# The first tap of the feed-forward convolution, for the first token group, on ScalarE out of PSUM

## The chip, the cores and the metric

One core of a Trainium2 chip. The metric is the device time of one launch in microseconds; lower is better. The kernel is written by hand, engine by engine, with semaphores between the engines; nothing reorders it afterwards.

## The reference, cut to what matters

Two decoder layers run over 1024 prompt tokens and 32 sample tokens (8 sequences of 4). Each layer has a mixer, a norm, a feed-forward block with a causal convolution of width 3, and a norm. The second layer's mixer holds a sparse attention: an indexer scores keys, the best 256 per query are kept, and the rest is masked. The change touches the feed-forward block:

```
def causal_dwconv(ext, w):
    t = ext.shape[1] - (CONV_W - 1)
    out = ext[:, CONV_W - 1:] * w[CONV_W - 1]
    for j in range(CONV_W - 1):
        out = out + ext[:, j:j + t] * w[j]
    return out

def conv_ffn(x, hist, w_up, conv_w, conv_b, w_down):
    hu = x @ w_up
    ext = jnp.concatenate([hist, hu], axis=1)
    hc = causal_dwconv(ext, conv_w) + conv_b
    y = (jax.nn.silu(hc[..., :D_FF]) * hc[..., D_FF:]) @ w_down
    return y, ext[:, -(CONV_W - 1):]
```

D_MODEL is 1024 and D_FF is 2816, that is 22 chunks of 128 channels (FC in the kernel), each with a half that goes through silu (j = 0) and a half that multiplies it (j = 1). `w[2]` is the tap on the token itself, and it is the first that the kernel takes, with the bias.

## The kernel before, in words

**Layout and groups.** Channels lie on the 128 partitions and tokens along the row. The tokens form two groups: GA, the first 512 prompt tokens, and GB, the other 512 and the 32 samples (544 columns). GA runs through a feed-forward block in one pass, GB in the next. The four passes are numbered pz: 0 (layer 0, GA), 1 (layer 0, GB), 2 (layer 1, GA), 3 (layer 1, GB). Beside pass 0 runs the norm of GB, row by row. Beside pass 2 run group B's sample attention, the indexer's scores and top-k, and prompt attention heads in pairs.

**Slabs.** Weights are streamed in slabs of 128x1024 or less. SyncE loads them into a ring of three buffers RAW. ScalarE rounds a slab to the high part WH (split_high, L1029), called by `ahead`, two slabs before PE needs it. GpSimd subtracts to get the low part WL (L1448). PE makes three matmuls per chunk of 128 (high by high at L606, low by high at L607, high by low at L609) into one of two slots of PSUM, which alternate. It takes a slot again when `evac_done` of that slot says that it was emptied.

**One pass.** A pass has blocks of 4, 6, 6 and 6 chunks. A block has two up slabs for each chunk (j = 0, then j = 1) and then 8 down slabs, so 8 + 8, 12 + 8, 12 + 8 and 12 + 8 slabs, numbered 0 to 75 below. An up slab's result, 128 channels by 512 tokens, takes this way:

- ScalarE copies it from PSUM to a row `ext` (L1148), behind two columns of history, and this frees the slot. The rows are extB0 and extB1 in passes 0, 1 and 3, and extA0 and extA1 in pass 2.
- VectorE makes the three taps in `taps`: `cv = ext * w2 + bias` (L1725, TENSOR_SCALAR), then adds `ext * w0` and `ext * w1` (L1729 and L1731, SCALAR_TENSOR_TENSOR). In a trace a tap is a line cvA or cvB.
- With j = 1, ScalarE takes silu of the j = 0 half (L1155), VectorE multiplies the halves to hf (L1847), and in the next slab but one ScalarE rounds hf to HH or HHA (`hidden_high`, L1123) and VectorE keeps the rest in HL or HLA (L1835) for the down slabs.

The taps' numbers and the bias are in `fpar[:, 2 * c + j, 0:4]`, in memory on the chip. At the start of pass 0 ScalarE itself issues the loads of fpar0 and of fhist (the samples' history); VectorE waits for `fpar_in` before its first tap. fpar1, for layer 1, is loaded before the end of the second pass.

**Order.** Each engine has its own list of steps. `beside(s, 0)` and `beside(s, 1)` put other work in front of or behind a slab's own: the norm's rows in pass 0 (ScalarE L1116 and L1117 write XLF and XH from Z, VectorE L1814 scales, GpSimd L1492 subtracts and adds in Z), the indexer's R (ScalarE L1181 and L1183) and SC (GpSimd L1503), the top-k (VectorE L2038 and L2040) and the pair steps in pass 2. A pair step has the row maxima of two heads' scores (VectorE L2059), exponentials (ScalarE L1225), the reciprocal of their sums (VectorE L2064), the scaled probabilities PRB (ScalarE L1229), and PE's transposition of them (L870), which stands between two slabs in PE's list. ScalarE loads a table of functions (ACT_TABLE_LOAD) when silu and the exponential alternate.

Of the kernel before, what the change touches and what calls it, by code (L numbers as in the profile page):

```python
# [173 lines left out]
def build(nc, io):  # L174
    with ExitStack() as ctx:
# [354 lines left out]
        def ffn_blocks(pz):  # L530

            n, c, out = PASSES[pz], 0, []
            for nb in BLOCKS:
                out.append((n, nb, c))
                n, c = n + 2 * nb + KD, c + nb
            return out
# [481 lines left out]
        def _(act):  # L1018
# [106 lines left out]
            def ffn(pz, q_norm):  # L1125

                layer, gr = pz // 2, pz % 2
                ext, cv = ffn_place(pz)[0:2]
                if pz == 0:
                    act.wait_ge(mm_done, F0[0])  # L1130
                    act.dma_start(fpar0[:, :, :], io["fpar"][0]).then_inc(fpar_in, 16)
                    act.dma_start(fhist[:, :, :, :], io["fhist"][0]).then_inc(fpar_in, 16)
                if pz == 2:
                    act.wait_ge(sc_acc, 32)
                    act.wait_ge(edge_zero, 4)
                for n, nb, c0 in ffn_blocks(pz):
                    for q in range(nb):
                        c = c0 + q
                        for j in range(2):
                            s = n + 2 * q + j  # L1140
                            u = 2 * FC * pz + 2 * c + j
                            beside(s, 0)
                            ahead(s)
                            act.wait_ge(mm_done, s + 1)
                            act.wait_ge(conv_done, u + 1)
                            act.wait_ge(st_done, u + 1)
                            for dst, src_ in zip(group_parts(ext[s % 2], gr, HIST), slot_parts(s)):
                                ins = act.activation(dst, src_, ACT.Copy)  # L1148
                            ins.then_inc(evac_done[s % 2], 1)
                            if j == 0 and q:  # L1150
                                hidden_high(pz, q - 1, c - 1)
                            if j == 1:
                                act.wait_ge(conv_done, u + 2)
                                w = EXTG[gr] - HIST
                                act.activation(cv[0][:, 0:w], cv[0][:, 0:w], ACT.Silu).then_inc(silu_done, 1)  # L1155
                            beside(s, 1)
                    n += 2 * nb
                    hidden_high(pz, nb - 1, c0 + nb - 1)
                    for m in range(KD):
                        beside(n + m, 0)  # L1160
                        ahead(n + m)
                        if c0 + nb == FC:
                            square(q_norm, m)
                        beside(n + m, 1)
                if gr == GB:
                    act.wait_ge(st_done, 2 * FC * (pz + 1) + 2)
                    act.dma_start(io["o_fst"][layer], fst[:, :, :]).then_inc(fst_out, 16)
# [477 lines left out]
        def _(dve):  # L1645
# [73 lines left out]
                dve.tensor_tensor(cf[:, :], cf[:, :], U[:, g, :], ALU.mult).then_inc(gate_f, 1)  # L1719
                mix_rest(g)  # L1720

            def taps(row, out, w, taps_w, tap_sem, value, done):

                if len(taps_w) == 4:
                    dve.tensor_scalar(out, row[:, 2:2 + w], taps_w[2], taps_w[3], ALU.mult, ALU.add).then_inc(tap_sem, 1)  # L1725
                else:
                    dve.tensor_scalar(out, row[:, 2:2 + w], taps_w[2], None, ALU.mult).then_inc(tap_sem, 1)
                dve.wait_ge(tap_sem, value + 1)
                dve.scalar_tensor_tensor(out, row[:, 0:w], taps_w[0], out, ALU.mult, ALU.add).then_inc(tap_sem, 1)  # L1729
                dve.wait_ge(tap_sem, value + 2)  # L1730
                dve.scalar_tensor_tensor(out, row[:, 1:1 + w], taps_w[1], out, ALU.mult, ALU.add).then_inc(done, 1)  # L1731

            for jj in range(4):
                n = 8 + 3 * jj
                dve.wait_ge(mm_done, n + 2)
                wait_emptied(dve, n)
                dve.wait_ge(bstd, jj + 1)
                for dst, src_, c in zip(parts(bext, HIST), bank_parts((n + 1) % 2), parts(cf)):
                    ins = dve.tensor_tensor(dst, src_, c, ALU.mult)
                ins.then_inc(evac_done[(n + 1) % 2], 1)  # L1740
                wait_emptied(dve, n + 1)
                dve.wait_ge(bhist, jj + 1)
                taps(bext, bcv[:, :], CW, [bw[:, jj, t:t + 1] for t in range(3)], btap, 2 * jj, bconv)
                dve.wait_ge(bconv, jj + 2)
                dve.wait_ge(mm_done, n + 3)
                conv_parts = [bcv[:, 0:2 * TW].rearrange("p (c t) -> p c t", c=2), bcv[:, 2 * TW:NP],
                              sample_cols(bcv, 0, HIST + DEC, DEC, NP)]
                for dst, src_, c in zip(parts(cf), bank_parts(n % 2), conv_parts):
                    ins = dve.tensor_tensor(dst, src_, c, ALU.mult)
                ins.then_inc(evac_done[n % 2], 1)  # L1750
                mix_rest(4 + jj)
# [97 lines left out]
            def ffn(pz, q_norm):  # L1849
# [8 lines left out]
                for n, nb, c0 in ffn_blocks(pz):  # L1858
                    for q in range(nb):
                        c = c0 + q  # L1860
                        for j in range(2):
                            s, local = n + 2 * q + j, 2 * c + j
                            u = 2 * FC * pz + local
                            beside(s, 0)
                            wait_emptied(dve, s)
                            if gr == GB:
                                dve.wait_ge(ext_hist, 2 * FC * layer + local + 1)
                            if j == 0 and FC * pz + c:
                                dve.wait_ge(hmul, FC * pz + c)
                            taps(ext[j], cv[j][:, 0:w], w, [fpar[:, local, t:t + 1] for t in range(4)], tap, 2 * u, conv_done)  # L1870
                            if j == 0 and q:
                                hidden_rest(pz, q - 1, c - 1)
                            if j == 1:
                                hidden(pz, c)
                            beside(s, 1)
                    n += 2 * nb
                    hidden_rest(pz, nb - 1, c0 + nb - 1)
                    for m in range(KD):
                        beside(n + m, 0)
                        projected(n + m, m, c0 == 0, c0 == 0)  # L1880
                        if c0 + nb == FC:
                            summed(q_norm, m)
                        beside(n + m, 1)
# [421 lines left out]
```

## Time and profile before

| what | value |
|---|---|
| time, 3 runs | median 2978.38 us (2977.19 to 2985.26) |
| the profiled execution's own time | 2971.72 us |
| its span | 2969.7 us |
| PE busy | 2655.3 us (89%) |
| VectorE (DVE) busy | 1606.8 us (54%) |
| ScalarE (ACT) busy | 1078.2 us (36%) |
| GpSimd (POOL) busy | 1242.6 us (42%) |
| chain that ended last | PE 63%, DVE 16%, ACT 7%, issue 5%, POOL 4% |

Times in the trace are microseconds from the start of the span; the profiled execution's time is 2 us more than its span. Busy time is what an engine's instructions took, their stalls among it. "Chain that ended last" follows the program back from its last instruction, at each step to what released it. A row of a timeline gives an instruction's start, its duration, the engine and line, the operation and its tiles, and in brackets how long the engine was idle in front of it and what ended that. PEclk is the clock granted to PE as a share of 2.4 GHz.

### The profile page before, as it was taken

The page shows a single profiled execution, that of the slowest core. Times are in us where ns is not written, and L with a number is a line of the kernel's source. Part 1 is how long each engine was busy: PE and PEld are TensorE (multiplying, and loading weights), DVE is VectorE, ACT ScalarE, POOL GpSimd, SP SyncE. Part 2 cuts the span into 40 slices and gives each one's busy share as a digit, 9 for nine tenths or more (in the row PEclk, how much of TensorE's full clock was granted, in tenths as well). Part 3 has the DMA queues.
Part 4 walks back from the last instruction along what each step waited for, and adds up shares of the span by engine and source line. Part 5 has one row for each costly group of instructions (what it writes and reads, how often), then busy time and mean ns, then how long its engine had stood idle before and what let it go on. Part 6 is the DMA issues. An engine that isn't in the chain of part 4 may idle for free.

```text
span 2969.7 us, 39274 instructions
## 1 busy us (share of the span) xinstructions
PE 2655.3 (89%) x15720; PEld 2254.1 (76%) x15720; DVE 1606.8 (54%) x2392; ACT 1078.2 (36%) x1732; POOL 1242.6 (42%) x1026
## 2 busy tenths in 40 slices
PE   7989988999979999989879669797889898899997
PEld 7989876878879999857768434355566667799997
DVE  3332575354564334567763368588994434553434
ACT  2111343333333223343234253155354543432333
POOL 2212444444455555465323341154222224554554
PEclk9999998999989999989889779899999999899998
DMA  3101222323222222312211314331111113132232
GB/s 125 43 30 58 86 67 75 93 93 98 86 64 81 91 92 80 109 51 83 97 54 62 108 33 134 117 128 41 59 54 61 57 55 118 48 96 86 82 95 80
DMA packets 96096, 235.44 MB, mean 79 GB/s; under 512 B 10442, under 2 KB 31498, under 8 KB 95530
## 3 DMA queue, kind: packets, MB, share of 16 engines
q1 hardware_dynamic: 85344, 210.95, 22.6%
q10 hardware_dynamic: 10570, 21.97, 2.0%
q8 instruction: 125, 2.05, 0.3%
q14 instruction: 57, 0.47, 0.1%
HBM read 219.43 MB, written 13.45 MB: 78 GB/s over the span
## 4 chain that ended last, share of the span: by engine, by line
PE 63%; DVE 16%; ACT 7%; issue 5%; POOL 4%; DMA 2%; SPq 1%; ACTq 0%; DVEq 0%; POOLq 0%
PE PS L606 19%; PE PS L609 18%; PE PS L607 18%; DVE SC L2038 3%; POOL WL L1448 2%; DMA RAW<-in_slabs 2%; POOL SC L1503 2%; ACT WH L1029 1%; DVE m8b L2040 1%; PE PS L816 1%; PE PS L852 1%; PE PS L795 1%; ACT XH L1117 1%; PE PS L870 1%; DVE m8a L2040 1%
## 5 line engine op out<-in xcount | busy, mean ns | idle before, releaser
L1448 POOL TENSOR_TENSOR WL<-RAW,WH 128x1024 fp32r<-128x1024 f32 (+2 forms) x400 | 885.7, 2215 | 1571.8 <-ACT WH L1029 1571.4
L606 PE MATMUL PS<-XH,WH 128*128 128x272 f32 (+2 forms) x3312 | 1076.5, 335 | 70.4 <-POOL WL L1448 32.5
L607 PE MATMUL PS<-XL,WH 128*128 128x272 f32 (+2 forms) x3312 | 1055.6, 329 | 0.0
L609 PE MATMUL PS<-XH,WL 128*128 128x272 f32 (+2 forms) x3312 | 882.8, 329 | 0.0
L606 PEld LDWEIGHTS PS<-XH,WH 128*128 128x128 f32 x3312 | 639.1, 193 | 143.9 <-issue 47.4
L607 PEld LDWEIGHTS PS<-XL,WH 128*128 128x128 f32 x3312 | 639.2, 193 | 41.4 <-issue 1.7
L1029 ACT ACTIVATE WH<-RAW 128x1024 fp32r<-128x1024 f32 (+2 forms) x400 | 388.0, 970 | 771.2 <-DMA RAW<-in_slabs 764.6
L609 PEld LDWEIGHTS PS<-XH,WL 128*128 128x128 f32 x3312 | 567.9, 192 | 43.4
L1725 DVE TENSOR_SCALAR cvB<-extB,fpar 128x560 f32<-128x560 f32 (+1 forms) x132 | 109.2, 827 | 395.3 <-ACT extB L1148 392.4
L606 PE MATMUL PS<-HH,WH 128*128 128x272 f32 (+1 forms) x880 | 265.2, 316 | 25.5 <-POOL WL L1448 18.0
L607 PE MATMUL PS<-HL,WH 128*128 128x272 f32 (+1 forms) x880 | 262.8, 313 | 0.0
L609 PE MATMUL PS<-HH,WL 128*128 128x272 f32 (+1 forms) x880 | 218.4, 313 | 0.0
L606 PEld LDWEIGHTS PS<-HH,WH 128*128 128x128 f32 x880 | 169.0, 192 | 38.8 <-POOL WL L1448 21.9
L1768 DVE TENSOR_TENSOR Z<-Z,PS 128x512 f32<-128x512 f32 (+1 forms) x96 | 67.5, 704 | 221.9 <-PE PS L609 221.9
L607 PEld LDWEIGHTS PS<-HL,WH 128*128 128x128 f32 x880 | 168.8, 192 | 8.1
L1148 ACT ACTIVATE extB<-PS 128x240 f32<-128x240 f32 (+3 forms) x308 | 92.2, 362 | 177.9 <-PE PS L609 177.9
L609 PEld LDWEIGHTS PS<-HH,WL 128*128 128x128 f32 x880 | 146.8, 192 | 7.8
L1729 DVE SCALAR_TENSOR_TENSOR cvB<-extB,fpar,cvB 128x560 f32<-128x560 f32 (+1 forms) x132 | 111.4, 844 | 4.7
L1731 DVE SCALAR_TENSOR_TENSOR cvB<-extB,fpar,cvB 128x560 f32<-128x560 f32 (+1 forms) x132 | 108.1, 819 | 4.7
L1492 POOL TENSOR_TENSOR Z<-Z,sqb 128x512 f32<-128x512 f32 (+1 forms) x64 | 95.1, 1504 | 13.7 <-ACT sqb L1095 13.7
L1765 DVE SCALAR_TENSOR_TENSOR Z<-Z,PS 128x512 f32<-128x512 f32 (+1 forms) x64 | 45.0, 704 | 90.0 <-PE PS L609 89.1
L1116 ACT ACTIVATE XLF<-Z,lnp 128x512 f32<-128x512 f32 (+1 forms) x48 | 39.6, 826 | 147.7 <-DVE Z L1814 147.7
(281 smaller groups left out, 3328.7 us busy)
## 6 DMA issues: line engine op xcount, KB each, us to landing
RAW<-in_slabs SPq DMA_DIRECT2D x272, 512.0 KB, 3.5
RAW<-in_slabs SPq DMA_DIRECT2D x96, 384.0 KB, 3.0
RAW<-in_slabs SPq DMA_DIRECT2D x32, 256.0 KB, 2.9
KP<-in_ck SPq DMA_DIRECT2D x32, 256.0 KB, 3.2
VP<-in_cv SPq DMA_DIRECT2D x32, 256.0 KB, 2.9
xb_rows<-spill ACTq DMA_DIRECT2D x8, 272.0 KB, 2.1
Z<-xb_rows ACTq DMA_DIRECT2D x1, 2176.0 KB, 12.6
out_o_y<-Z ACTq DMA_DIRECT2D x4, 544.0 KB, 2.8
```

The source lines that it names most:

```text
L606: pe.matmul(o, WH[n % 3][:, k, :], hi(k)[:, c], start=first, stop=False)
L607: pe.matmul(o, WH[n % 3][:, k, :], lo(k)[:, c], start=False, stop=False)
L609: mm = pe.matmul(o, WL[n % 3][:, k, :], hi(k)[:, c], start=False, stop=last)
L1029: act.activation(WH[n % 3][:, 0:kc, :], RAW[n % 3][:, 0:kc, :], ACT.Copy).then_inc(w_hi, 1)
L1148: ins = act.activation(dst, src_, ACT.Copy)
L1448: pool.tensor_tensor(WL[n % 3][:, 0:kc, :], RAW[n % 3][:, 0:kc, :], WH[n % 3][:, 0:kc, :].bitcast(F32), ALU.subtract).then_inc(w_lo, 1)
L1492: pool.tensor_tensor(z, z, LNS[q][3][:, :], ALU.subtract).then_inc(ln_sub, 1)
L1725: dve.tensor_scalar(out, row[:, 2:2 + w], taps_w[2], taps_w[3], ALU.mult, ALU.add).then_inc(tap_sem, 1)
L1729: dve.scalar_tensor_tensor(out, row[:, 0:w], taps_w[0], out, ALU.mult, ALU.add).then_inc(tap_sem, 1)
L1731: dve.scalar_tensor_tensor(out, row[:, 1:1 + w], taps_w[1], out, ALU.mult, ALU.add).then_inc(done, 1)
L1768: dve.tensor_tensor(by_bank(z, gr), by_bank(z, gr), slot(n), ALU.add).then_inc(evac_done[n % 2], 1)
L2038: dve.match_replace(SC[b], m8[x][:, :], SC[b], TAKEN).then_inc(top_, 1)
```

## The change

For the groups GA (passes 0 and 2, 88 up slabs) ScalarE makes the first tap itself. Right behind its copy of a slab's result it reads the same slot of PSUM once more and writes `cv[j] = slot * w2 + bias` as an Identity activation whose scale and bias are read from fpar. It waits first for `hmul`, so that the last chunk's halves in cv have been multiplied, and the slot is freed by this second instruction. For that ScalarE waits for `fpar_in` ahead of each such pass. VectorE makes the two other taps only; `taps` is cut in two. Passes 1 and 3 keep all three taps on VectorE.

```
                 ext, cv = ffn_place(pz)[0:2]
+                fpar = (fpar0, fpar1)[layer]
                 if pz == 0:
                     act.wait_ge(mm_done, F0[0])
...
+                if gr == GA:
+                    act.wait_ge(fpar_in, 48 if layer else 32)
                 for n, nb, c0 in ffn_blocks(pz):
...
                                 ins = act.activation(dst, src_, ACT.Copy)
+                            if gr == GA:
+                                act.wait_ge(hmul, FC * pz + c)
+                                ins = act.activation(cv[j][:, 0:HALF], slot(s), ACT.Identity,
+                                                     scale=fpar[:, 2 * c + j, 2:3], bias=fpar[:, 2 * c + j, 3:4])
                             ins.then_inc(evac_done[s % 2], 1)
...
-            def taps(row, out, w, taps_w, tap_sem, value, done):
+            def first_tap(row, out, w, taps_w, tap_sem, value):
 
                 if len(taps_w) == 4:
                     dve.tensor_scalar(out, row[:, 2:2 + w], taps_w[2], taps_w[3], ALU.mult, ALU.add).then_inc(tap_sem, 1)
                 else:
                     dve.tensor_scalar(out, row[:, 2:2 + w], taps_w[2], None, ALU.mult).then_inc(tap_sem, 1)
-                dve.wait_ge(tap_sem, value + 1)
+                dve.wait_ge(tap_sem, value)
+
+            def other_taps(row, out, w, taps_w, tap_sem, value, done):
+
                 dve.scalar_tensor_tensor(out, row[:, 0:w], taps_w[0], out, ALU.mult, ALU.add).then_inc(tap_sem, 1)
-                dve.wait_ge(tap_sem, value + 2)
+                dve.wait_ge(tap_sem, value)
                 dve.scalar_tensor_tensor(out, row[:, 1:1 + w], taps_w[1], out, ALU.mult, ALU.add).then_inc(done, 1)
...
-                            taps(ext[j], cv[j][:, 0:w], w, [fpar[:, local, t:t + 1] for t in range(4)], tap, 2 * u, conv_done)
+                            taps_w = [fpar[:, local, t:t + 1] for t in range(4)]
+                            if gr == GB:
+                                first_tap(ext[j], cv[j][:, 0:w], w, taps_w, tap, 6 * FC * layer + 2 * FC + 2 * local + 1)
+                            other_taps(ext[j], cv[j][:, 0:w], w, taps_w, tap,
+                                       6 * FC * layer + (local + 1 if gr == GA else 2 * FC + 2 * local + 2), conv_done)
```

How it moves instructions on ScalarE at the start of pass 0, before and then with the change (fpar_99 is fpar0, WH_61 the high part of slab 2, extB_102 the row of slab 0, cvB_104 its taps):

```order
L1131 DMA fpar_99<-in_fpar 128x176 [waits slab_multiplied]
L1132 DMA fhist<-in_fhist 128x704
L1029 ACTIVATE WH_61<-RAW_55 128x1024 [waits slab_loaded2]
L1148 ACTIVATE extB_102<-PS 128x512 [waits ffn_state,ffn_conv,slab_multiplied]
L1095 ACTIVATE sqb_214<-PS 128x544 [waits squares_summed,ln_mean_spread]
L1101 ACTIVATE stats<-stats,epst 68x8 [waits ln_var]
```

```order
L1132 DMA fpar_99<-in_fpar 128x176 [waits slab_multiplied]
L1133 DMA fhist<-in_fhist 128x704
L1029 ACTIVATE WH_61<-RAW_55 128x1024 [waits slab_loaded2,ffn_params_in]
L1151 ACTIVATE extB_102<-PS 128x512 [waits ffn_state,ffn_conv,slab_multiplied]
L1154 ACTIVATE cvB_104<-PS,fpar_99 128x512 [waits ffn_hidden]
L1095 ACTIVATE sqb_214<-PS 128x544 [waits squares_summed,ln_mean_spread]
L1101 ACTIVATE stats<-stats,epst 68x8 [waits ln_var]
```

The wait for the parameters (ffn_params_in) stands in front of the split of slab 2, and the tap behind the copy.

ScalarE around a pair step in the last block of pass 2, slab 58 (extA_160 is its row, HHA_201 the first rounded hidden row of the block, PRB the pair's probabilities), before and then with the change:

```order
L1029 ACTIVATE WH_59<-RAW_53 128x1024 [waits slab_loaded0]
L1148 ACTIVATE extA_160<-PS 128x512 [waits ffn_state,ffn_conv,slab_multiplied]
L1123 ACTIVATE HHA_201<-hfA 128x512 [waits ffn_hidden]
L1225 ACT_TABLE_LOAD [waits pa_turned]
L1225 ACTIVATE PRB,psm<-PS,nmx 128x896 [waits pa_max]
```

```order
L1029 ACTIVATE WH_59<-RAW_53 128x1024 [waits slab_loaded0]
L1151 ACTIVATE extA_160<-PS 128x512 [waits ffn_state,ffn_conv,slab_multiplied]
L1154 ACTIVATE cvA_162<-PS,fpar_154 128x512 [waits ffn_hidden]
L1123 ACTIVATE HHA_201<-hfA 128x512 [waits ffn_hidden]
L1232 ACT_TABLE_LOAD [waits pa_turned]
```

The tap stands ahead of the hidden row's rounding and of the table load for the exponentials; it and the rounding wait for the same semaphore (ffn_hidden is hmul).

VectorE around the pair step at slab 40 (SC_158 are the indexer's scores, m8a and m8b the maxima that the top-k takes out), before and then with the change:

```order
L2040 MAX m8b<-SC_158 128x8 [waits i_top]
L2059 TENSOR_REDUCE nmx<-PS 128x1 [waits pa_logits] x2
L1725 TENSOR_SCALAR cvA_162<-extA_160,fpar_154 128x512 [waits ffn_hidden,banks_emptied0]
L1729 SCALAR_TENSOR_TENSOR cvA_162<-extA_160,fpar_154,cvA_162 128x512 [waits ffn_tap]
L1731 SCALAR_TENSOR_TENSOR cvA_162<-extA_160,fpar_154,cvA_162 128x512 [waits ffn_tap]
L1835 TENSOR_TENSOR HLA<-hfA,HHA_202 128x512 [waits ffn_hidden_high]
L2064 RECIPROCAL prc<-psm 128x1 [waits pa_exp] x2
```

```order
L2056 MAX m8b<-SC_158 128x8 [waits i_top]
L2075 TENSOR_REDUCE nmx<-PS 128x1 [waits pa_logits] x2
L1739 SCALAR_TENSOR_TENSOR cvA_162<-extA_160,fpar_154,cvA_162 128x512 [waits ffn_hidden,banks_emptied0]
L1741 SCALAR_TENSOR_TENSOR cvA_162<-extA_160,fpar_154,cvA_162 128x512 [waits ffn_tap]
L1847 TENSOR_TENSOR HLA<-hfA,HHA_202 128x512 [waits ffn_hidden_high]
L2080 RECIPROCAL prc<-psm 128x1 [waits pa_exp] x2
```

One instruction is gone between the row maxima and the reciprocals; the others keep their order.

## Rows read from the trace of the kernel before

**Rows 1.** Stretches: window, us; busy PE, PEld, DVE, ACT, POOL; PEclk.
```profile
405.00:460.00 55.00, 40.82 (x148) 31.01 (x148) 38.29 (x38) 21.20 (x32) 23.21 (x20) 0.85 0.13 43
2130.00:2250.00 120.00, 97.69 (x485) 70.42 (x485) 109.72 (x164) 60.43 (x90) 30.97 (x24) 0.91 0.16 51
2250.00:2410.00 160.00, 147.44 (x786) 108.66 (x783) 57.99 (x90) 84.74 (x125) 43.99 (x31) 0.97 0.18 57
```

**Rows 2.** PE's waits, 2030 to 2250, then 2250 to 2430: us, times, longest.
```profile
PE PS L870 <- ACT PRB L1229: 31.0, 8, 6.2
...
PE PS L870 <- ACT PRB L1229: 15.1, 6, 3.1
```

**Rows 3.** Groups by form, DVE and ACT: busy us, mean ns | idle before.
```profile
L1725 DVE TENSOR_SCALAR cvA<-extA,fpar 128x512 f32<-128x512 f32 x44 | 32.7, 742 | 63.2 <-ACT extA L1148 63.2
...
L1148 ACT ACTIVATE extA<-PS 128x512 f32<-128x512 f32 x44 | 26.2, 595 | 79.6 <-PE PS L609 79.6
...
L1117 ACT ACTIVATE XH<-Z,lnp 128x512 fp32r<-128x512 f32 x24 | 19.2, 800 | 0.0
```

**Rows 4.** Timelines of POOL and DVE in the row loop: start, duration, instruction.
```profile
433.68 2.35 POOL L1448 TENSOR_TENSOR WL<-RAW,WH 128x1024 fp32r<-128x1024 f32 x1 [5.20 <-ACT WH L1029]
...
436.32 1.36 POOL L1492 TENSOR_TENSOR Z<-Z,sqb 128x544 f32<-128x544 f32 x1
...
424.94 2.19 DVE L1725 TENSOR_SCALAR cvB<-extB,fpar 128x512 f32<-128x512 f32 x1 [2.44 <-ACT extB L1148]
...
434.12 2.20 DVE L1725 TENSOR_SCALAR cvB<-extB,fpar 128x512 f32<-128x512 f32 x1 [2.44 <-ACT extB L1148]
436.36 1.87 DVE L1729 SCALAR_TENSOR_TENSOR cvB<-extB,fpar,cvB 128x512 f32<-128x512 f32 x1
```

**Rows 5.** Timelines of ACT and PE around slab 58 of pass 2.
```profile
2313.95 0.60 ACT L1148 ACTIVATE extA<-PS 128x512 f32<-128x512 f32 x1 [3.83 <-PE PS L609]
2314.44 0.63 ACT L1123 ACTIVATE HHA<-hfA 128x512 fp32r<-128x512 f32 x1
...
2318.36 1.97 ACT L1229 ACTIVATE PRB<-PRB,prc 128x896 f32<-128x896 f32 x2
...
2319.45 0.98 PE L870 MATMUL PS<-ident,PRB 128*128 128x128 f32 x7 [2.75 <-ACT PRB L1229]
```

**Rows 6.** Timelines of DVE and PE at the start of pass 0.
```profile
396.26 0.55 DVE L1725 TENSOR_SCALAR cvB<-extB,fpar 128x512 f32<-128x512 f32 x1 [2.82 <-DMA fhist<-in_fhist]
396.85 0.75 DVE L1729 SCALAR_TENSOR_TENSOR cvB<-extB,fpar,cvB 128x512 f32<-128x512 f32 x1
...
399.65 0.72 DVE L1803 SCALAR_TENSOR_TENSOR sqa<-ident,stats 68x544 f32<-68x544 f32 x1
...
400.65 1.08 PE L676 MATMUL PS<-sqa,onesd 68*128 68x272 f32 x4
```

**Rows 7.** Timelines of ACT and POOL at slab 18 of pass 2 (scores).
```profile
1965.21 0.58 ACT L1148 ACTIVATE extA<-PS 128x512 f32<-128x512 f32 x1
...
1969.89 2.51 POOL L1503 TENSOR_TENSOR SC<-SC,R 128x896 f32<-128x896 f32 x1 [0.21 <-ACT R L1183]
```

**Rows 8.** Timelines of DVE and PE around slab 40 of pass 2.
```profile
2169.88 0.54 DVE L1725 TENSOR_SCALAR cvA<-extA,fpar 128x512 f32<-128x512 f32 x1
...
2172.51 0.21 DVE L2064 RECIPROCAL prc<-psm 128x1 f32<-128x1 f32 x2
...
2173.69 1.54 PE L870 MATMUL PS<-ident,PRB 128*128 128x128 f32 x6 [6.21 <-ACT PRB L1229]
```

**Rows 9.** Stretches after two waits (PE busy, PEclk), then PE's timeline at two transpositions.
```profile
2317.90:2324.70 6.80, 5.25 (x30) 1.00 0.08 11
2345.20:2352.00 6.80, 5.92 (x18) 0.50 0.00 0
...
2346.08 1.97 PE L870 MATMUL PS<-ident,PRB 128*128 128x128 f32 x8 [3.06 <-ACT PRB L1229]
...
2404.54 1.09 PE L870 MATMUL PS<-ident,PRB 128*128 128x128 f32 x8 [3.07 <-ACT PRB L1229]
```

More of the change, by code:

```diff
@@ L1742, in _ @@
                 dve.wait_ge(bhist, jj + 1)
-                taps(bext, bcv[:, :], CW, [bw[:, jj, t:t + 1] for t in range(3)], btap, 2 * jj, bconv)
+                taps_w = [bw[:, jj, t:t + 1] for t in range(3)]
+                first_tap(bext, bcv[:, :], CW, taps_w, btap, 2 * jj + 1)
+                other_taps(bext, bcv[:, :], CW, taps_w, btap, 2 * jj + 2, bconv)
                 dve.wait_ge(bconv, jj + 2)
```

## The prediction

> **What bounds the kernel now.** I read the page first: the matrix engine is busy for 89% of the span, and of the chain that ended last 63% is PE, 16% DVE and 7% ACT. So most of the program is bound by PE, and a tap that moves from DVE to ACT can only matter where PE waits. The table of stretches then shows where that is [rows 1]: in the start of the first pass PE is busy for 40.8 of 55 us, in the middle of the third pass for 97.7 of 120 while DVE is busy for 109.7 (91%), and in the last block of that pass PE has 147 of 160 us and DVE only 58. Everywhere else in the two passes that the change touches PE is kept busy slab after slab, and neither DVE nor ACT is what it waits for. The list of PE's waits names the engine that ends them in the third pass: ScalarE's normalised probabilities PRB, 31.0 us in 8 waits and 15.1 us in 6 [rows 2]. ScalarE is where the change adds work, so each wait has to be read by what is late inside the chain in front of PRB.
>
> **The tap itself.** A tap of 512 columns costs DVE a mean of 742 ns in the third pass [rows 3], 0.55 us where nothing disturbs it (the next instruction starts 0.58 us later) and 2.20 us beside a GpSimd operation [rows 4]. On ScalarE it does not exist yet. The nearest row is the norm's activation with a scale and a shift from memory, 128x512, 800 ns from SBUF; the copy out of PSUM, 595 ns, is the lower bound [rows 3]. I take 0.78 us. Back to back, a ScalarE instruction starts about 0.1 us before the one ahead is shown to end (2314.44 against 2313.95 + 0.60 [rows 5]), so the queue behind the tap moves by **0.69 us** (bounds 0.5 to 0.8). The row then becomes ready for DVE's second tap at copy + 1.3 us, where it now takes copy + 1.2. The bank is released by the tap and not by the copy, 0.7 us later; no PE wait in the trace is ended by the copy, so this costs nothing, and the cover is the second bank, into which PE works meanwhile.
> The Trainium skill, "ScalarE: Activation LUTs", section "Rules for kernel authors", says to put mul and add on VectorE and not on ScalarE, and so speaks against this change; its section "What ACT_TABLE_LOAD costs" prices an activation with two pointers at about 0.80 us for 512 columns, by my estimate. If each of the 88 taps were on the chain, 0.69 for 0.58 would give +9.7 us; the rows below show that only some are, so I follow the rows.
>
> **Start of pass 0: +1.7.** ScalarE itself issues the loads of fpar and fhist, and DVE's first tap waits 2.82 us for the second, until 396.26 [rows 6]. Now ScalarE waits there too, with the split WH of slab 2, the copy and the tap queued behind the wait, one after the other (1.0 + 0.5 + 0.8 us): DVE's second tap starts at about 398.5, not 396.85. Behind it on DVE stand the norm's statistics up to sqa (399.65), and PE takes sqa at 400.65 with no idle time before it [rows 6]. So PE gets a new wait of 1.7 us. Bounds: 0, if PE has work in hand that covers it, and +1.7. The same wait in layer 1 is for a load that the whole second pass and more lies behind; it costs nothing.
>
> **The row loop of pass 0, slabs 2 to 7: -2.7.** Here norm and up-projection form one loop: split, copy, DVE tap, two more taps, gating or rest, norm scaling, XH on ScalarE, split. It takes 9.2 us per slab (the tap starts at 424.94 and the next at 434.12 [rows 4]). The tap takes 2.20 us, from 434.12 to 436.32, because GpSimd subtracts WL from 433.68 to 436.03; the second tap takes 1.87, to 438.23, because GpSimd's Z runs from 436.32 to 437.68 [rows 4]. Without the tap on DVE, the second tap would start at about 434.9, end behind WL at about 436.8, and it is the third that then stands against Z, until 437.68 + 0.75 = 438.4 instead of 439.0: 0.6 us gained per slab, in slabs 3, 4 and 5; 0.5 in the shorter 6 and 7; 0.1 lost in slab 2, where the tap was not stalled. Sum -2.7. Bounds: 0, if the stall only goes to the next instruction in full; -5.2, if most of the 2.2 us goes with the tap.
> The Trainium skill, "SBUF — State Buffer", section "Who interferes with whom", has it that of DVE and GpSimd the loser blocks for the whole instruction; it would give the -2.7, while sharing of bandwidth would give nearer the -5.2. The rows agree with blocking.
> From slab 8 on to the end of pass 0, PE is bound by its own work: nothing.
>
> **Scores, slabs 17 to 24 of pass 2 (1955 to 2030): +0.9.** GpSimd's SC and ScalarE's R alternate there. From 1965.21 on the copy, the hidden copy and R stand in front of SC at 1969.89, which waited 0.21 us for R [rows 7]: +0.69 once, +0.2 at the next one; in the others ScalarE has 0.6 to 0.7 us to spare. Bounds -2 (stalls of DVE beside GpSimd that go) and +4 (each of six slabs).
>
> **Pair steps where DVE is full (slabs 25 to 42): -2.1.** The wait at slab 40, 6.21 us, is typical: DVE's row maxima, its tap at 2169.88, two more taps, the rest HLA, the reciprocals at 2172.51, PRB, PE at 2173.69 [rows 8]. ScalarE is idle in front of its exponentials, so its own tap is free, and two removed taps give 1.16 against 0.1 for the hand-over: -1.1. The same gives -0.6 at slab 25 and -0.5 at slab 27 (one tap each); at slab 37 ScalarE's own chain holds the exponentials, +0.1. The waits at down slabs have no tap. Bounds: 0, and 8 taps by 0.58 = -4.6.
>
> **Pair steps where ScalarE is last (slabs 43, 46, 58, 61, 64, 67): +4.1.** At slab 58 the copy is at 2313.95, the probabilities start at 2318.36 without idle time between, and PE has waited 2.75 us at 2319.45 [rows 5]. The tap lies in that chain: 6 x 0.69 = +4.1. DVE's saving there is worth nothing: its reciprocal waits for ScalarE.
>
> **Clock: +1.7.** Around the end of a wait of 3.06 us, at 2346.08, PE's granted clock is 0.50 (1.2 GHz) for 6.8 us; around the end of the 2.75 us at slab 58 it stays 1.00 (2.4 GHz) [rows 9]. A half-clock stretch of 6.8 us costs 3.4. Three of the six lengthened waits have none now. I take half of one more; bounds -3 and +10.
>
> **Sum:** 1.7 - 2.7 + 0.9 - 2.1 + 4.1 + 1.7 = **+3.6 us**. The profiled execution took 2971.7 us, so 2975.3; the median of the runs is 6.7 above it (2978.38), and there I say **2982.0**. A difference of 0.3%, 9 us, is about what a measurement of this kernel can tell from none.
>
> **Rivals.**
> *The clock falls* (slower, 0.25). The added 0.69 us brings all six waits to 3.2 us or more, and PE comes back at half clock from the three that are now spared: 3 x 3.4 in place of my 1.7 gives +12.1, 2990.5. For it: the two cases lie only 0.3 us of waiting apart [rows 5, 9]. Against: behind another wait of 3.07 us the same eight transposing matmuls take 1.09 us in all, not 1.97 [rows 9]. It decides from the second new stretch on.
> *DVE's relief carries on* (faster, 0.15). If the freed time shifts everything behind it (8 x 0.58 = -4.6, the loop -5.2, scores -2), and ScalarE's +4.1 and the start's +1.7 are partly covered (say +2.4 left), the sum is -9.4: 2969. For it: DVE at 91%. Against: that PE's waits end at ScalarE in the majority of steps. The Trainium skill, "Perfetto Trace Analysis", section "Optimizing Scalar/DVE Operations", suggests handing work to Scalar where DVE is saturated; the row on 2130 to 2250 agrees with the condition, that on 2250 to 2410 does not.
> *Nothing on the path* (0.15): the waits lengthen where PE's next wait then shrinks, and gains and losses cancel: 2978.
> The forecast itself has 0.45. Together with the third rival that is 0.60 within 0.3%. The range runs from 2967 (all low bounds but a few) to 2995 (the forecast with its high bounds on clock and scores).
>
> **What would show it.** Right: a tap of 0.75 to 0.82 us on ScalarE; a PE wait of 1.7 us before the norm's spread at about 402; a loop period of 8.6 instead of 9.2; six PRB waits longer by 0.69; that of 6.21 down to about 5.1. Wrong: more than one new half-clock stretch; PE waits that end at the bank's release; a second tap that gains the whole 2.2 us; an unchanged 2.75 before 2319, with ScalarE's chain covered.

## The result and the profile after

The change takes 2986.37 us (median of 7 runs, 2984.22 to 2991.24), the kernel before 2977.19 beside it (7 runs). The ratio is 1.0033, with a 95% interval of 1.0019 to 1.0047: **slower**, by a third of a per cent or 10 us, between 6 and 14. The two profiled executions lie farther apart than the medians, 2971.7 and 2989.4 us, so the traces show where the time goes, and the medians how much it is.

The page of the changed kernel, busy times and the chain that ended last:

```profile
PE 2661.3 (89%) x15720; PEld 2260.6 (76%) x15720; DVE 1531.8 (51%) x2304; ACT 1135.5 (38%) x1820; POOL 1246.7 (42%) x1026
...
PE 63%; DVE 15%; ACT 8%; issue 5%; POOL 4%; DMA 3%; SPq 1%; ACTq 0%; DVEq 0%; POOLq 0%
```

DVE is relieved of 75 us and ACT has 57 more, and the program is longer. The stretches that answer to [rows 1], as long as the same work now takes (window, us; busy PE, PEld, DVE, ACT, POOL; PEclk):

```profile
410.00:466.00 56.00, 42.72 (x158) 32.55 (x158) 33.55 (x34) 24.57 (x38) 24.37 (x20) 0.87 0.14 47
2137.00:2261.00 124.00, 100.44 (x483) 72.54 (x484) 103.56 (x152) 67.51 (x101) 30.91 (x24) 0.89 0.15 48
2261.00:2427.00 166.00, 150.16 (x785) 110.49 (x782) 50.11 (x78) 92.70 (x137) 44.12 (x31) 0.95 0.17 55
```

In the last one PE's granted clock is 0.95, where it was 0.97, and about the same work (785 matmuls for 786) takes 166 us, where it took 160.

**The tap on ScalarE** in pass 2, from the view of one tile's instructions (ns min/median/max, first and last start):

```profile
L1154 ACT ACTIVATE cvA<-PS,fpar x44: 766/772/777, 1772.5 to 2414.1; 128x512 f32<-128x512 f32 x44
```

It takes 0.77 us, against the 0.78 forecast.

**The pair step at slab 58**, ACT and then PE, to be read beside [rows 5]:

```profile
2325.38 0.60 ACT L1151 ACTIVATE extA<-PS 128x512 f32<-128x512 f32 x1 [4.01 <-PE PS L609]
2325.87 0.77 ACT L1154 ACTIVATE cvA<-PS,fpar 128x512 f32<-128x512 f32 x1
2326.53 0.63 ACT L1123 ACTIVATE HHA<-hfA 128x512 fp32r<-128x512 f32 x1
2327.18 1.28 ACT L1232 ACT_TABLE_LOAD   x1
...
2330.46 1.97 ACT L1236 ACTIVATE PRB<-PRB,prc 128x896 f32<-128x896 f32 x2
...
2331.55 1.61 PE L870 MATMUL PS<-ident,PRB 128*128 128x128 f32 x7 [3.41 <-ACT PRB L1236]
...
2341.08 1.09 PE L887 MATMUL PS<-PTB,VT 128*64 128x128 f32 x16 [0.61 <-ACT PTB L1248]
```

Copy to PRB takes 5.08 us, where it took 4.41, and PE's wait is 3.41, where it was 2.75: +0.66, as forecast. The last row was not forecast. PE waits a second time in this step, for PTB, ScalarE's copy of the transposed probabilities, which it did not before. In slab 59 ScalarE's chain of copy, tap, table load and silu stands in front of PTB:

```profile
2336.95 0.60 ACT L1151 ACTIVATE extA<-PS 128x512 f32<-128x512 f32 x1 [1.84 <-PE PS L609]
2337.45 0.77 ACT L1154 ACTIVATE cvA<-PS,fpar 128x512 f32<-128x512 f32 x1
2338.24 1.28 ACT L1162 ACT_TABLE_LOAD   x1
2339.53 0.63 ACT L1162 ACTIVATE cvA<-cvA 128x512 f32<-128x512 f32 x1
2340.07 0.96 ACT L1248 ACTIVATE PTB<-PS 128x512 f32<-128x512 f32 x2
```

PE's wait for PTB of about 0.61 us comes four times, behind slabs 41, 47, 59 and 65, each time where a j = 1 slab has its silu and so its table load.

**The pair step at slab 40**, beside [rows 8]:

```profile
2179.41 1.54 PE L870 MATMUL PS<-ident,PRB 128*128 128x128 f32 x6 [5.12 <-ACT PRB L1236]
```

6.21 us has become 5.12, as forecast (5.1).

**The start of pass 0**: ACT, POOL, DVE and PE, beside [rows 6]:

```profile
396.56 1.06 ACT L1029 ACTIVATE WH<-RAW 128x1024 fp32r<-128x1024 f32 x1 [4.30 <-DMA fhist<-in_fhist]
397.52 0.58 ACT L1151 ACTIVATE extB<-PS 128x512 f32<-128x512 f32 x1
398.00 0.77 ACT L1154 ACTIVATE cvB<-PS,fpar 128x512 f32<-128x512 f32 x1
...
397.69 2.41 POOL L1455 TENSOR_TENSOR WL<-RAW,WH 128x1024 fp32r<-128x1024 f32 x1 [8.61 <-ACT WH L1029]
...
398.91 1.74 DVE L1739 SCALAR_TENSOR_TENSOR cvB<-extB,fpar,cvB 128x512 f32<-128x512 f32 x1 [5.12 <-ACT cvB L1154]
...
403.47 2.18 PE L676 MATMUL PS<-sqa,onesd 68*128 68x272 f32 x4 [2.34 <-DVE sqa L1815]
```

The new wait is there, and longer than the 1.7 us forecast: the delayed split also delayed GpSimd's WL (397.69 to 400.10), and VectorE's tap now runs into it and takes 1.74 us instead of 0.75. After the wait PE comes back slowly (window, us, PE busy, PEclk):

```profile
405.00:410.50 5.50, 5.50 (x15) 0.54 0.00 0
```

**Where the time went, by PE's progress.** PE's list is the same in all kernels of this study, so the n-th matmul of two traces can be set side by side (the traces of e1 to e4 and e9 to e11 lack the records of 20 matmuls, which are skipped). The table gives its start with the change, or in an experiment below, minus its start in the kernel before, at nine places (times of the kernel before, us).

| place | change | e1 | e2 | e3 | e4 | e5 | e6 | e7 | e8 | e9 | e10 | e11 |
|---|---|---|---|---|---|---|---|---|---|---|---|---|
| 398, before the norm's spread | +0.3 | -0.1 | +1.6 | -0.1 | +0.8 | +0.9 | +0.8 | +1.1 | +0.7 | +1.9 | +2.3 | +2.0 |
| 427, behind the start of pass 0 | +5.2 | +5.0 | +2.1 | -0.8 | +0.1 | +0.9 | 0.0 | +1.8 | +0.4 | +2.3 | +2.8 | +1.8 |
| 472, behind the row loop | +3.4 | +3.3 | +2.2 | -2.8 | -1.9 | +1.0 | -1.8 | +1.5 | -1.6 | +2.4 | +2.5 | 0.0 |
| 490, in the down slabs | +3.5 | +3.4 | +2.2 | -3.9 | -2.8 | +1.1 | -1.8 | +0.4 | -2.6 | +2.2 | +1.4 | +1.4 |
| 1950, in pass 2 before the scores | +7.7 | +3.9 | +3.1 | -3.3 | -1.2 | +2.1 | +2.0 | +2.3 | -1.4 | +2.8 | +3.4 | +3.7 |
| 2030, behind the scores | +9.2 | +4.0 | +4.7 | -1.7 | -0.9 | +2.1 | +3.6 | +2.4 | -1.4 | +2.8 | +3.4 | +4.0 |
| 2190, behind the steps where DVE is full | +7.0 | +3.7 | +2.3 | -3.6 | -2.8 | +2.1 | +1.0 | +2.5 | -1.9 | +2.6 | +3.5 | -0.4 |
| 2440, behind the last pair step | +17.2 | +6.3 | +12.4 | +6.6 | -6.7 | +14.5 | +4.5 | +14.8 | -3.4 | +8.4 | +8.6 | +2.6 |
| end | +18.0 | +7.6 | +15.3 | +7.6 | -2.8 | +15.4 | +5.3 | +16.1 | -1.8 | +9.1 | +12.9 | +4.2 |

For the change that is +3.2 in the start and row loop of pass 0, +1.5 in the scores, -2.2 where DVE is full, +10.2 from 2190 to 2440, and +5.3 in the rest, of which 4.2 between 490 and 1950, and 4.1 of these between 1200 and 1763, which lies in neither of the two passes. How much such a rest can be worth is seen from 2190 to 2440 in kernels whose taps there are those of the kernel before: +2.6 in e1, -1.5 in e8 and -3.9 in e4.

The +10.2 from 2190 to 2440 are in about equal parts waits and slower matmuls. The same stretch of PE's work, before and then with the change:

```profile
2190.00:2440.00 250.00, 221.98 (x1187) 0.95 0.17 54
2197.00:2457.15 260.15, 226.87 (x1186) 0.93 0.16 52
```

PE is idle for 28.0 and then 33.3 us (+5.3), and busy for 222.0 and 226.9 (+4.9) with the same matmuls, at a lower mean clock.

### The profile page after: what moved, and what is told of

Its sections match the earlier page's. It is cut to its first block, busy times and chain, and to the rows that moved or that the text cites. A ratio compares the mean times of both kernels' runs of the same rounds, so it can differ in the third digit from the quotient of the medians.

```text
span 2987.7 us, 39276 instructions
## 1 busy us (share of the span) xinstructions
PE 2661.3 (89%) x15720; PEld 2260.6 (76%) x15720; DVE 1531.8 (51%) x2304; ACT 1135.5 (38%) x1820; POOL 1246.7 (42%) x1026
## 4 chain that ended last, share of the span: by engine, by line
PE 63%; DVE 15%; ACT 8%; issue 5%; POOL 4%; DMA 3%; SPq 1%; ACTq 0%; DVEq 0%; POOLq 0%
PE PS L606 19%; PE PS L607 18%; PE PS L609 18%; DVE SC L2054 2%; POOL WL L1455 2%; DMA RAW<-in_slabs 2%; POOL SC L1510 2%; ACT WH L1029 1%; PE PS L852 1%; DVE m8b L2056 1%; PE PS L816 1%; PE PS L795 1%; ACT XH L1117 1%; PE PS L870 1%; DVE m8a L2056 1%
## 5 line engine op out<-in xcount | busy, mean ns | idle before, releaser
L1732 DVE TENSOR_SCALAR cvB<-extB,fpar 128x560 f32<-128x560 f32 x88 | 61.2, 696 | 282.8 <-ACT extB L1151 282.8
L1739 DVE SCALAR_TENSOR_TENSOR cvB<-extB,fpar,cvB 128x560 f32<-128x560 f32 (+1 forms) x132 | 110.8, 839 | 163.0 <-ACT cvB L1154 159.9
L1741 DVE SCALAR_TENSOR_TENSOR cvB<-extB,fpar,cvB 128x560 f32<-128x560 f32 (+1 forms) x132 | 114.8, 869 | 4.7
```

## The experiments

All of them decide slab by slab on which engine the first tap is made. Their lists differ from the change in one condition, and the semaphore values are counted accordingly:

```
+def on_act(pz, local):
+    return ...
...
-                            if gr == GA:
+                            if on_act(pz, 2 * c + j):
+                                act.wait_ge(fpar_in, 48 if layer else 32)
                                 act.wait_ge(hmul, FC * pz + c)
```

`local` counts the 44 up slabs of a pass from 0 (slabs 16 to 27 are local 8 to 19, 36 to 47 are 20 to 31, 56 to 67 are 32 to 43). VectorE makes the first tap where `on_act` is false. The wait ahead of a whole pass stays only where slab 0 of that pass is ScalarE's. In their profiles line numbers are 9 to 13 higher than those of the change (L881 is L870, L898 is L887).

| run | taps on ScalarE | median us | ratio to before, 95% |
|---|---|---|---|
| e1 | pass 0 | 2975.16 | 0.9996 (0.9987 to 1.0005) |
| e2 | pass 2 | 2985.86 | 1.0032 (1.0020 to 1.0044) |
| e3 | both, without chunk 0 of pass 0 | 2982.65 | 1.0024 (1.0015 to 1.0032) |
| e4 | where VectorE is late | 2969.23 | 0.9978 (0.9970 to 0.9987) |
| e5 | ten slabs of pass 2 | 2988.91 | 1.0043 (1.0030 to 1.0057) |
| e6 | both, without the ten and chunk 0 | 2973.68 | 0.9984 (0.9975 to 0.9993) |
| e7 | the ten, and again on VectorE | 2988.64 | 1.0045 (1.0031 to 1.0058) |
| e8 | pass 0, wait at the tap | 2971.34 | 0.9985 (0.9976 to 0.9994) |
| e9 | six of the ten | 2981.43 | 1.0017 (1.0008 to 1.0026) |
| e10 | four of the ten | 2982.27 | 1.0021 (1.0012 to 1.0030) |
| e11 | e8's pass 0 and e4's pass 2 | 2968.59 | 0.9973 (0.9962 to 0.9984) |

The kernel before had medians of 2975.68 (beside e1 to e4), 2976.4 (e5 to e8) and 2976.5 us (e9 to e11). Gains and losses in us below are differences of these medians or come from the ratio; the two agree within 2.1 us, and intervals are those of the ratio.

### Which pass loses: e1, e2, e3, e4

```
e1:  return pz == 0
e2:  return pz == 2
e3:  return pz == 2 or pz == 0 and local >= 2
e4:  return pz == 0 and 2 <= local < 8 or pz == 2 and 16 <= local < 25
```

> ScalarE takes the first tap in pass 0 only (44 slabs); pass 2 is as before. Theory A (both passes lose): the trace of the change shows a new 2.3 us wait of PE at the norm's spread, a half-clock stretch behind it, and a row loop that wins back about 2.4 us, net +3.4 us over the kernel before. Theory B (only the start of pass 0 loses, pass 2 cancels out): the whole difference of about 9 us stands here. Theory C (only pass 2 loses): 0.

> ScalarE takes the first tap in pass 2 only; pass 0 is as before. Theory A: the remainder, about +6 us over the kernel before, with six waits for PRB longer by 0.6 to 0.7 us and four new waits of 0.6 us for PTB. Theory B: 0. Theory C: the whole 9 us.

> As the change, but the two slabs of chunk 0 in pass 0 keep their first tap on VectorE, so that ScalarE does not wait for the parameters at the pass's start. Theory A: PE's 2.3 us wait at the norm's spread and the half-clock stretch at 406 are gone, 5.8 us less than the change, +3.4 over the kernel before. Theory B: 9 us less than the change, equal to the kernel before. Theory C: as the change.

> ScalarE takes the first tap only where VectorE is on the chain: slabs 2 to 7 of pass 0 (the row loop) and, of pass 2, slabs 24 to 27 and 36 to 40; VectorE keeps it elsewhere. Theory A: -2.4 us in pass 0 and -3 to -5 in pass 2, so 5 to 7 us faster than the kernel before. Theory B: -2.4 in pass 0 and 0 in pass 2. Theory D (the tap on ScalarE is worth nothing anywhere): 0.

Measured: pass 0 alone makes no difference (between -4 and +1.5 us), pass 2 alone loses 9.5 us (6 to 13), the whole of it. So theory B falls, and C stands nearer than A; e3 at +7 us (4.5 to 9.5) lies between what the two said. But pass 0 is not idle. From 398 to 472 in the table, e3, without chunk 0 on ScalarE, gains 2.7 us, and e1 loses 5.1 at the start, up to 427, and regains about 1.8 behind it. By the times the start of e1 loses about what the row loop gains; by the one trace it loses more. And e4 is faster than the kernel before by 0.22%, 6.5 us, as theory A had it: the tap on ScalarE is worth something where VectorE is late. In e4, PE's waits between 2030 and 2190 are (us in total, times, longest):

```profile
PE PS L881 <- ACT PRB L1248: 23.6, 6, 5.1
PE PS L617 <- DVE HLA L1859: 3.6, 1, 3.6
```

In the kernel before the same two rows are 26.0 (6, 6.2) and 4.1.

### Which slabs of pass 2 lose: e5, e6, e7, e9, e10

```
e5:  return pz == 2 and local in (25, 27, 30, 31, 34, 35, 37, 40, 41, 43)
e6:  return pz == 0 and local >= 2 or pz == 2 and local not in (25, 27, 30, 31, 34, 35, 37, 40, 41, 43)
e9:  return pz == 2 and local in (27, 30, 34, 37, 40, 43)
e10: return pz == 2 and local in (25, 31, 35, 41)
e7:  as e5, and VectorE
-                            if not on_act(pz, local):
+                            if True:
                                 first_tap(
```

> ScalarE takes the first tap in ten slabs of pass 2 alone: 43, 46, 58, 61, 64, 67 (in front of a pair's exponentials) and 41, 47, 59, 65 (in front of a pair's second PTB copy). Theory A1 (the loss of the change is ScalarE's chain in these ten slabs, with what the clock does behind the longer waits): 6 x 0.67 + 4 x 0.6 = +6.4 us by the waits alone, up to +10 with the clock, and the other 78 taps are not a loss. Theory A2 (the loss is spread, each tap costs a little): a tenth to an eighth of it, about +1.

> As the change, without those ten slabs and without the two of chunk 0 in pass 0: 76 taps on ScalarE. Theory A1: a gain like that of the run with taps only where VectorE is late, 5 to 7 us faster than the kernel before. Theory A2: still slower than the kernel before by 5 us or more.

> As e5_ten_slabs, but VectorE makes the first tap of the ten slabs as well, again, behind ScalarE's; so ScalarE's work is added and nothing is taken from VectorE. If VectorE's relief is worth nothing in these slabs, the waits of PE and the time are those of e5_ten_slabs; if it is worth its 0.58 us, each of the six waits is longer by that and the time by 3.5 to 6 us.

> ScalarE takes the first tap in slabs 43, 46, 58, 61, 64 and 67 of pass 2 alone, in front of a pair's exponentials. Theory W (what the ten slabs lose is their waits; the clock only follows by chance): 6 x 0.65 = +3.9 us over the kernel before, no wait for PTB. Theory K (most of it is half-clock stretches that longer waits bring): +8 us or more, with at least 15 more matmuls at half clock between 2190 and 2450 than in the run with taps only where VectorE is late.

> ScalarE takes the first tap in slabs 41, 47, 59 and 65 of pass 2 alone, in front of a pair's second PTB copy. Theory W: four new waits of 0.6 us for PTB, +2.4 us, and the PRB waits as in the kernel before. Theory K: such short waits bring no half-clock stretch, so +2.4 as well. If these slabs cost nothing, the kernel before's time and no wait.

Ten slabs out of 88 lose 12.5 us (9 to 17), at least as much as the whole change (6 to 14). The other 76 taps without chunk 0 gain 2.7 by the medians and 4.8 by the ratio (2 to 7; e6), less than the 5 to 7 of theory A1, but a gain; A2 falls. Making the ten taps a second time on VectorE costs nothing: e7 takes as long as e5, and PE's wait at slab 58 is 3.41 us in both. So in these slabs VectorE's relief is worth nothing and ScalarE's tap costs its full length. PE's waits from 2190 to 2450 in e5:

```profile
PE PS L881 <- ACT PRB L1248: 23.8, 8, 3.8
PE PS L863 <- DVE MB L2073: 6.6, 1, 6.6
PE PS L898 <- ACT PTB L1260: 3.4, 4, 1.5
```

and in e4, where these slabs are VectorE's:

```profile
PE PS L881 <- ACT PRB L1248: 20.3, 8, 3.1
PE PS L863 <- DVE MB L2073: 6.4, 1, 6.4
...
PE PS L898 <- ACT PTB L1260: 1.5, 1, 1.5
```

The waits for PRB and PTB are 3.5 + 1.9 = 5.4 us longer in e5, and with the wait behind slab 41, 0.61 us at 2184.85, which lies before that window, 6.0. The forecast of the waits alone was 6.4. e9 has six waits longer by 0.6 to 0.7 and no new one for PTB, e10 four new waits of 0.6 and its PRB waits are as before: each of the two groups does what was said of it. The times go beyond the waits: 4.9 us for 3.9 (e9), 5.8 for 2.4 (e10), 12.5 for 6.0 to 6.4 (e5). What stands beside that in the profiles is the granted clock. The stretch of e5 that answers to 2190 to 2440 of the kernel before, shown above, is

```profile
2192.10:2454.50 262.40, 228.64 (x1187) 0.93 0.16 51
```

PE is idle for 33.8 us, where it was 28.0 (+5.7, the waits), and busy for 228.6 with the same matmuls, where it was 222.0 (+6.7, the clock). So in this pair of profiles about half of the loss is the clock's. From slab 41 to the last pair step, the work takes 246 us at a mean clock of 0.95 in the kernel before, 243 at 0.97 in e4, 249 at 0.94 in e1, 252 at 0.95 in e9, 252 at 0.94 in e10, 258 at 0.93 in e5 and 256 at 0.93 with the change.

The waits are those of theory W. Of the times, e9's (2.4 to 7.7 us) holds W's 3.9 and ends just short of K's 8. e10's (3.6 to 8.9) holds neither theory's 2.4: what its other 3 to 4 us are was not found. K's sign, at least 15 more slow matmuls than in e4, is there in e9 (43 of the matmuls of 512 columns take 0.54 us or more between 2190 and 2450, 14 in e4), but the kernel before has 28 and e10 also 43, so it does not tell the theories apart.

The length of a wait does not by itself decide whether the clock falls to half (0.50, 1.2 GHz). In e1, PE's wait at slab 58 is the same 2.75 us as before [rows 5], and yet (PE's row, and window, us, PE busy, PEclk)

```profile
2324.14 1.09 PE L881 MATMUL PS<-ident,PRB 128*128 128x128 f32 x7 [2.75 <-ACT PRB L1248]
...
2323.90:2330.70 6.80, 6.56 (x29) 0.75 0.07 9
```

where [rows 9] have 1.00 around the same transposition. In e9, waits of 3.41 and 3.73 us bring no half clock:

```profile
2325.69 0.98 PE L881 MATMUL PS<-ident,PRB 128*128 128x128 f32 x7 [3.41 <-ACT PRB L1248]
2352.98 1.09 PE L881 MATMUL PS<-ident,PRB 128*128 128x128 f32 x8 [3.73 <-ACT PRB L1248]
...
2325.00:2332.00 7.00, 6.31 (x35) 1.00 0.21 69
2352.00:2359.00 7.00, 6.02 (x35) 1.00 0.14 51
```

What tips it was not found. But it is not chance alone. In the five kernels with all ten taps on ScalarE (the change, e2, e3, e5, e7) each of the six waits for PRB has a half-clock stretch at it, 30 of 30; in the six with none of them (before, e1, e4, e6, e8, e11) it is 20 of 36, and 4 of 6 in e9 and in e10. Over all profiles of that work the mean clock is 0.92 to 0.94 in those five kernels and 0.94 to 0.97 in those six. And the mean clock over a whole execution, which is on record for every run, averages 0.943 to 0.945 in the five (34 executions), 0.946 in the kernel before (the 73 beside the experiments) and 0.946 to 0.949 in the other five of the six (51). So the ten taps go with a lower clock on the average: by about 0.02 in that stretch, or 5 us of 250 by my estimate. In a single execution chance is as large.

### What the start loses: e8

```
e1:  return pz == 0
e8:  return pz == 0, and
-                if on_act(pz, 0):
-                    act.wait_ge(fpar_in, 48 if layer else 32)
                 for n, nb, c0 in ffn_blocks(pz):
```

> ScalarE takes the first tap in pass 0 only, as in e1_pass0_only, but its wait for the parameters stands right in front of the first tap, behind the split and the copy. Theory S1 (the start lost 2.8 us because the split and the copy queue behind the wait, and because GpSimd's subtraction, moved with the split, then stalls VectorE's next tap): PE's wait at the norm's spread shrinks from 2.4 to under 0.8 us, the half-clock stretch at 406 is gone, and the time is 2 to 4 us below the kernel before. Theory S2 (the tap itself, made late on ScalarE, is the loss): the wait stays above 1.5 us, and the time is that of e1_pass0_only.

S1. With the wait behind the split and the copy, ACT, DVE and PE of e8 are

```profile
393.84 0.58 ACT L1160 ACTIVATE extB<-PS 128x512 f32<-128x512 f32 x1
397.05 0.78 ACT L1164 ACTIVATE cvB<-PS,fpar 128x512 f32<-128x512 f32 x1 [2.63 <-DMA fhist<-in_fhist]
...
397.97 0.75 DVE L1749 SCALAR_TENSOR_TENSOR cvB<-extB,fpar,cvB 128x512 f32<-128x512 f32 x1 [3.81 <-ACT cvB L1164]
...
401.56 1.18 PE L687 MATMUL PS<-sqa,onesd 68*128 68x272 f32 x4
```

PE does not wait at the norm's spread, VectorE's tap is 0.75 us long and not 1.74, and PE's clock is 1.00 from 401 to 406: theory S1. e8 is 0.15% faster than the kernel before (4.5 us, between 2 and 7) and 3.8 us below e1, though the two intervals overlap (e1: -4 to +1.5). In the traces e1 loses 5.1 us from 398 to 427, the change 4.9, and e8 gains 0.3. So the place of one wait is worth at least what the whole row loop gains.

### A version that beats both: e11

```
e11: return pz == 0 or pz == 2 and 16 <= local < 25      (the wait as in e8)
```

> ScalarE takes the first tap in all of pass 0, with the wait for the parameters right in front of the tap, and in slabs 24 to 27 and 36 to 40 of pass 2. If the gains add up: 4 us in pass 0 and 2 to 3 in pass 2, 6 to 7 us under the kernel before. If the row loop's gain needs chunk 0 on VectorE: 2 to 3 us only.

Measured: 0.9973, 8 us below the kernel before (between 5 and 11). That is what was said for gains that add up (6 to 7), and not the 2 to 3 of the other case. It is not told apart from either half: e4, which differs only in pass 0 (chunk 0 and blocks 1 to 3 on VectorE), and e8, which has no tap on ScalarE in pass 2, have intervals that overlap with its own.

## Why the prediction was right or wrong

The direction and the range held: +3.6 us was forecast, about +10 measured, and 2986.4 lies between 2967 and 2995. The range reaches from the faster rival to beyond the slower one, so that it held says little. The size is too small by a factor of nearly three: the time lies just past the 0.3% that were called no change (0.33%, the interval on both sides of it), where the forecast's own case put it within, and halfway between the forecast's 2982.0 and the 2990.5 of the rival "the clock falls". Three terms were too small: the start of pass 0, the second half of the pair steps, which was put at nothing, and the clock.

- **The tap, +0.69 on ScalarE's queue: right.** 0.77 us long, next instruction 0.66 us after its start. The Trainium skill, "ScalarE: Activation LUTs", section "Rules for kernel authors", speaks against mul and add on ScalarE; my estimate by its section "What ACT_TABLE_LOAD costs" gave 0.80, the trace has 0.77. The sum of +9.7, with all 88 taps on the chain, is near the time measured, but not for its reason: 76 of the taps are no loss (e6).
- **Pair steps where ScalarE is last, +4.1: right for the waits that it counted, and a path left out.** The six waits for PRB grew by 3.9 us (+0.66 at slab 58; e9). The step counted only the first half of a pair step. The second half has a chain of its own, copy, tap, table load, silu, PTB, which had just fitted before in slabs 41, 47, 59 and 65; four waits of 0.61 us were missed, +2.4 (e10). The kernel before shows no row of a wait there; the slack had to be worked out as for the first half.
- **Clock, +1.7: mis-sized.** The step took half of one more half-clock stretch. The change has three more, at the waits that were spared (at 2236, 2332 and 2421), and the three that were there stay, that near 2377 before among them: its eight transposing matmuls take 1.95 us before and 1.97 with the change. Stretches behind two of the new ones, and then the transposition of 2377, before and with the change:

```profile
2331.50:2335.00 3.50, 3.46 (x12) 0.54 0.00 0
2421.00:2424.50 3.50, 3.50 (x13) 0.58 0.00 0
...
2375.88 1.95 PE L870 MATMUL PS<-ident,PRB 128*128 128x128 f32 x8 [3.07 <-ACT PRB L1229]
2390.35 1.97 PE L870 MATMUL PS<-ident,PRB 128*128 128x128 f32 x8 [3.73 <-ACT PRB L1236]
```

  So the prediction's own sign of being wrong, more than one new half-clock stretch, came true, and the rival "the clock falls" had it right. Its 12.1 us were too many: the new stretches are about 3.5 us long and not 6.8. From 2190 to 2440 PE's matmuls take 4.9 us longer with the change and 6.7 in e5. Its condition, that waits of 3.2 us and more bring one, does not hold: e9 has 3.41 and 3.73 without, and waits of the same 2.75 us have it both ways.
- **Start of pass 0, +1.7: too small.** The new wait is 2.34 us. What the step left out is that the split's delay moves GpSimd's WL onto VectorE's tap (1.74 for 0.75 us). PE then works at half clock for about 5 us, which was counted for pass 2 only. The start costs 4.9 us in the trace of the change (398 to 427 in the table), and the wait's place is worth 3.8 by the times of e1 and e8.
- **Row loop, -2.7: about right.** From 398 to 472 in the table, the five kernels whose start loses nothing gain 2.0 to 2.7 us (e3, e4, e6, e8, e11). The period fell as said: from 9.2 to 8.7 (the change's taps on ScalarE start at 430.23 and 438.89). The stall passes to the next instructions, as the step said: L1739 and L1741 of the change are 1.79 and 1.87 us long there, where the three taps before took 2.20, 1.87 and 0.75:

```profile
431.03 1.79 DVE L1739 SCALAR_TENSOR_TENSOR cvB<-extB,fpar,cvB 128x512 f32<-128x512 f32 x1 [3.10 <-ACT cvB L1154]
432.86 1.87 DVE L1741 SCALAR_TENSOR_TENSOR cvB<-extB,fpar,cvB 128x512 f32<-128x512 f32 x1
```

  What follows up to 490 is the clock's: another 1.0 to 1.1 us gained in e3, e4 and e8, nothing in e6, 1.4 lost in e11, and 1.1 gained too in e7 and e10, whose pass 0 is that of the kernel before.
- **Scores, +0.9: right in sign, 1.5 measured** (1.6 in e2, 0 in e1 and e8, where ScalarE has no tap there).
- **Pair steps where DVE is full, -2.1: the number came out, in part by luck.** It is -2.2 between 2030 and 2190, and slab 40 is at 5.12. But PE's idle time there fell by 4.4 us and its busy time rose by 2.2, at a lower clock. Before, and then with the change:

```profile
2030.00:2190.00 160.00, 128.14 (x627) 0.89 0.17 53
2039.20:2197.00 157.80, 130.34 (x626) 0.87 0.17 54
```

  The waits at down slabs, said to be unchanged, fell too: that for PRB at 2038.8 before is 3.9 us long, and 1.4 with the change.
- **Where PE waits.** The first step had neither VectorE nor ScalarE as what PE waits for in the rest of the two passes. From 1763 to 2030 the trace of the kernel before has 6.1 us of waits for ScalarE's R and 3.6 for VectorE's HLA.
- **The faster rival** asked for relief that carries on, 9.4 us of it. There is a gain, of 3 to 8 us, in e4, e6 and e11, where ScalarE is spared the ten slabs; in the change the ten slabs outweigh it. The rival "nothing on the path" falls with the ratio's interval. The advice of the Trainium skill to hand work to Scalar where DVE is saturated ("Perfetto Trace Analysis", section "Optimizing Scalar/DVE Operations") is borne out for slabs 24 to 27 and 36 to 40, where the six traces with these taps gain about 2 to 4 us between 2030 and 2190 and the six without them 0.5 at most, and not for those behind, though DVE was 91% busy over 2130 to 2250.

## What to carry to other kernels

Busy shares say which engine is full, but what a moved instruction is worth is decided step by step, by which engine's chain ends last in front of the wait: here ten slabs of 88 cost at least what the change lost, and the rest of it, without the two taps of the start, was a gain (e6). For the receiving engine, look at every result that it hands on behind the new instruction, the ones without a wait too, since a slack of less than 0.1 us (the tap moves the chain by 0.66, PE waits 0.61) shows in no list of waits. And a wait added to an in-order queue belongs right in front of the first instruction that needs it: moving it over one split and one copy gave back about 4 us.

## What was not expected of the hardware

PE's granted clock over the same 246 us of work, from slab 41 to the last pair step, is 0.94, 0.95 and 0.97 in three kernels that have the same instructions there (e1, before, e4), a difference of 6 us between the last and the first, with PE's waits for PRB there equal to 0.2 us. This is as large as the effects sought, and large enough that two profiles can lie 18 us apart where the medians lie 9 to 10: what one pair of profiles shows of a stage has to be compared with the same stage in kernels that did not alter it.
